# Order on TensorE in the attention steps: the product with the values of step k-1 placed behind the turning of the probabilities of step k

## The chip, the cores and the metric

One NeuronCore of a Trainium2 chip (TensorE, VectorE, ScalarE, GpSimd and SyncE, with 16 DMA engines) runs the whole kernel in one launch. The metric is device time in microseconds (us). In the profile TensorE is PE (its weight loads are PEld), VectorE is DVE, ScalarE is ACT, GpSimd is POOL and SyncE is SP. L12 is line 12 of the kernel.

## The reference

A decoder block for 256 tokens of width 1024, in float32: RMSNorm, one wide projection, a Mamba-2 mixer beside a sparse attention with 16 heads of width 64, a merge of the two by gates, an output projection, and a top-4-of-32 mixture of experts with a final RMSNorm. The part of the attention that the change touches is this:

```python
p_sel = masked_softmax(jnp.einsum('bqgrd,bgqmd->bgrqm', qb, kg), smask)
o_sel = jnp.einsum('bgrqm,bgqmd->bqgrd', p_sel.astype(vg.dtype), vg)
...
p_win = masked_softmax(jnp.einsum('bqgrd,bkgd->bgrqk', qb, kw), wmask)
o_win = jnp.einsum('bgrqk,bkgd->bqgrd', p_win.astype(vw.dtype), vw)
...
o = g[..., 0, None] * o_cmp + g[..., 1, None] * o_sel + g[..., 2, None] * o_win
```

With 256 tokens the eight chosen blocks of 64 and the window of 256 both cover all earlier tokens, so both branches are plain causal attention, with keys and values of their own.

## The kernel before

Five engines run fixed instruction streams and meet at semaphores. Up to the mixture of experts, all streams are written from one hand-made list, `token_order()`: a list of pairs (kind, number). PE, ACT, DVE and POOL each go through the whole list in its order and issue what that kind means for them; an engine that has nothing to do for a kind skips it. The place of a pair in the list therefore sets the order on four engines at once.

The attention is 16 steps k. Step k handles one tile of 128 queries (t = k // 8) and two heads. For t = 0 (k = 0 to 7) there are 128 keys, for t = 1 (k = 8 to 15) there are 256. The kinds are:

- `SC k`, the scores. PE multiplies queries and keys (L930, eight matmuls, banks 3 and 4). DVE scales, masks and takes the maxima (L1749, four custom instructions) and negates them (L1754). ACT takes the exponentials with their sums (L1342, four). PE's `SC k` waits for DVE's L1754 of `SC k-1`. The probabilities lie in one of three buffers, named TH or XDT in the rows.
- `RW k`, the row weights. DVE works out the factors from sums and gates (L1758, L1760, L1763) and POOL multiplies the probabilities with them (L661).
- `PT k`, the turning. PE transposes the probabilities (L711, four or eight matmuls) into banks 5 and 6, after POOL's L661. ACT copies bank 5 (L1350) and DVE bank 6 (L1771) into the one buffer `PTS`. PE's `PT k` also waits for both copies of step k-1.
- `PV k`, the product with the values. PE multiplies (L961 and L967) from `PTS` into bank 7. ACT writes the rounded part (L1354, OTH) and DVE the rest (L1502, OTL), which frees bank 7.
- `H u` and `P u`, the two halves of a projection unit u (24 matmuls of 256 columns each, L757 and L760), which fill PE between the attention's own instructions.
- `W u` prepares the weights of a later unit: ACT copies them rounded (L1184, WH), and POOL (L621, for the units of the merge gates and of the SSM branch) or DVE (L1472, for the others) writes what the rounding left over (WL). In these steps a `W` stands right behind an `H`.
- `GR 0` (ACT) and `GX 0` (DVE L1706, eight instructions) in steps 0 and 1, and `YS 0` (ACT L1213, DVE L1498) in step 4, finish the SSM branch.

Two waits tie `PTS` down, since it exists once. The copies of step k wait until PE has read step k-1 out of it:

```python
if k >= 1:
    act.wait_ge(pv_full, k)
a(PTS[:, 0, 0:n], psum[:, 5, 0:n], ACT.Copy).then_inc(pt_act, 1)
```

and `PV k` waits for the copies of step k (`pt_act` and `pt_dve` at k + 1) and for `pv_read` at k, the freeing of bank 7.

When the sixteenth OTL is written (`pv_read` at 16), ACT issues nine small loads (`LD 0`, L1204 to L1210) and goes on with the weights of the next units, PE starts on the NSA branch projection (`H 37`), and SP may issue the first load of expert weights (`first_load(0)`). From about 400 us to the end the mixture of experts runs, which streams 403 MB of weights.

Of the kernel before, what the change touches and what calls it, by code (L numbers as in the profile page):

```python
# [81 lines left out]
def token_order():  # L82


    u = {x: n for n, x in enumerate(UNITS)}
    out = []

    def unit(kind, m=0):
        out.extend([("H", u[(kind, m)]), ("P", u[(kind, m)])])

    for m in range(8):
        unit("xbc", m)
        if m >= 1:
            out.append(("F", m - 1))
    unit("small")
    out += [("F", 7), ("XD", 0), ("DT", 0)]
    unit("kc")
    out += [("S1", 0)]
    unit("vc")
    out += [("XT", 0)]  # L100
    unit("ks")
    out += [("XT", 1)]
    unit("kw")
    out += [("HID", 0), ("BT", 0), ("A", 0)]
    unit("vs")
    out += [("HT", 0), ("A", 1), ("XT", 2)]
    unit("vw")
    out += [("K2", 0), ("Y", 0), ("A", 2), ("ST", 0), ("XT", 3)]
    for m in range(4):
        unit("q", m)  # L110
        out += [("Y", m + 1), ("A", m + 3)]
        if m == 0:
            out += [("ST", 1)]
    unit("z", 0)
    out += [("Y", 5), ("A", 7)]
    unit("z", 1)
    out += [("Y", 6)]
    unit("z", 2)
    out += [("Y", 7), ("V2", 0), ("CT", 0), ("GY", 0)]
    unit("z", 3)  # L120
    out += [("CS", 0), ("GY", 1)]
    unit("mg", 0)
    out += [("GN", 0), ("CP", 0), ("GY", 2), ("SC", 0)]
    unit("mg", 1)
    out += [("GN", 1), ("GY", 3), ("SC", 1)]
    halves = []
    for x in [("mg", m) for m in range(2, 8)] + [("bs", m) for m in range(4)]:
        halves += [("H", u[x]), ("P", u[x])]
    out += [halves.pop(0), ("GN", 2), halves.pop(0), ("GN", 3)]
    for k in range(17):  # L130

        if k + 2 < 16:
            out.append(("SC", k + 2))
        if k < 16:
            out.append(("RW", k))
        out += {0: [("GR", 0)], 1: [("GX", 0)], 4: [("YS", 0)]}.get(k, [])
        if halves and k in (1, 8):
            out.append(halves.pop(0))
        if k >= 1:
            out.append(("PV", k - 1))  # L140
        if halves:
            out.append(halves.pop(0))
        if k < 16:
            out.append(("PT", k))
    out += halves + [("LD", 0)]
    for m in range(4):
        unit("bn", m)
        if m >= 1:
            out.append(("MT", m - 1))
    out.append(("MT", 3))  # L150
    for m in range(4):
        out.append(("H", u[("wo", m)]))
        if m:
            out.append(("XX", m - 1))
        out.append(("P", u[("wo", m)]))
        if m:
            out.append(("RM", m - 1))


    order, due = [("W", SPLIT_UNITS[SPLITS - 1])], []  # L160
    first, last = out.index(("GR", 0)), out.index(("PT", 15))
    for n, token in enumerate(out):
        order.append(token)
        if token[0] == "H" and token[1] in SPLIT_UNITS[1:]:
            i = SPLIT_UNITS.index(token[1]) - 1 + SPLITS
            if i < len(SPLIT_UNITS):
                due.append(("W", SPLIT_UNITS[i]))
        if not first <= n < last or token[0] in ("H",):
            order += due
            due = []  # L170
    return order


TOKENS = token_order()


# [1793 lines left out]
```

## Time and profile before

| | |
|---|---|
| Device time, median of 3 runs | 1339.52 us (1335.58 to 1339.84) |
| Device time of the profiled execution | 1334.48 us |
| Its span, first to last instruction | 1332.8 us |
| PE busy | 1234.6 us, 93% |
| DVE, ACT, POOL busy | 444.1, 282.3, 149.0 us |
| Mean granted PE clock | 0.981 of full speed |
| Attention steps, from the start of `PT 0` to the last OTL | 209.7 us to 336.7 us |

Busy time is the time in which an engine had an instruction in work. All places in the trace are in us from the start of the span. The profiled execution is one of its own, shorter than the median of the three runs.

### The profile page before, as it was taken

Reading aid. Unit: us, or ns where it says so; the run is one execution under the profiler, and the core shown is the slowest. Engines: PE = TensorE matmul, PEld = TensorE weight load, DVE = VectorE, ACT = ScalarE, POOL = GpSimd, SP = SyncE. Lnnn points to the kernel's source line nnn. Section 1 sums busy time; section 2 is a strip of 40 time slices with the busy share of each in tenths; the row PEclk is TensorE's granted clock in tenths of the full one; section 3 lists DMA queues with packets and bytes.
Section 4 is the critical chain, followed back from the end, with each engine's and each line's share of the span. In section 5 each row is a group of like instructions: output and inputs, shape, how many; then the busy total and the mean of one; then the engine's idle time right before and its main releaser. Section 6 shows DMA issues by size and latency. Waiting matters only on the chain.

```text
span 1332.8 us, 17482 instructions
## 1 busy us (share of the span) xinstructions
PE 1234.6 (93%) x7089; PEld 661.9 (50%) x7089; DVE 444.1 (33%) x902; ACT 282.3 (21%) x507; POOL 149.0 (11%) x101
## 2 busy tenths in 40 slices
PE   7999996898899999999999898998989899898985
PEld 7999986777884443434434233332423333232321
DVE  6965446455633131221212213121221212122113
ACT  4673444453331010101101011010101001010001
POOL 1301345353630000000000000000000000000000
PEclk9999997899999999999999999999999999999998
DMA  7747433112698999999999999999999999999994
GB/s 239 209 129 228 127 106 116 64 64 95 236 363 342 395 432 426 430 427 430 427 430 427 428 428 428 430 427 430 427 430 427 431 427 430 427 428 429 426 428 205
DMA packets 79964, 454.08 MB, mean 341 GB/s; under 512 B 10160, under 2 KB 53296, under 8 KB 55344
## 3 DMA queue, kind: packets, MB, share of 16 engines
q1 hardware_dynamic: 76960, 451.30, 82.9%
q10 hardware_dynamic: 2960, 2.17, 0.6%
q8 instruction: 31, 0.51, 0.2%
q14 instruction: 13, 0.11, 0.0%
HBM read 452.40 MB, written 1.05 MB: 340 GB/s over the span
## 4 chain that ended last, share of the span: by engine, by line
PE 60%; DMA 31%; DVE 6%; ACT 1%; issue 1%; ACTq 1%; POOL 0%; DVEq 0%; SPq 0%
DMA ring<-in_w_gate_up_dram 28%; PE psum L1043 19%; PE psum L1057 10%; PE psum L757 9%; PE psum L760 7%; PE psum L1032 5%; PE psum L1083 3%; DMA ring<-in_w_down_dram 3%; PE psum L711 2%; DVE AMX L1754 1%; PE psum L930 1%; DVE YV L1706 1%; DVE WL L1472 1%; PE psum L967 1%; PE psum L1014 1%
## 5 line engine op out<-in xcount | busy, mean ns | idle before, releaser
L1043 PE MATMUL psum<-ring,ZS 128*64 128x512 f32 x1504 | 355.2, 616 | 14.2 <-DMA ring<-in_w_gate_up_dram 14.2
L1043 PEld LDWEIGHTS psum<-ring,ZS 128*64 128x64 f32 x1504 | 100.0, 134 | 230.3 <-issue 192.5
L1906 DVE TENSOR_TENSOR X<-X,psum 128x1024 f32<-128x1024 f32 x64 | 75.3, 1217 | 388.7 <-PE psum L1083 388.7
L1057 PE MATMUL psum<-ring,HT 128*64 128x512 f32 x784 | 176.6, 596 | 20.3 <-DMA ring<-in_w_down_dram 19.6
L1890 DVE TENSOR_SCALAR ZS<-psum 128x512 f32<-128x512 f32 x32 | 22.1, 692 | 315.1 <-PE psum L1043 315.1
L1043 PE MATMUL psum<-slot,ZS 128*64 128x512 f32 x528 | 123.8, 615 | 2.0 <-DMA slot<-in_w_gate_up_dram 2.0
L1057 PEld LDWEIGHTS psum<-ring,HT 128*64 128x64 f32 x784 | 54.4, 136 | 129.9 <-issue 104.0
L1391 ACT ACTIVATE HT<-psum 128x512 f32<-128x512 f32 x32 | 19.1, 597 | 324.3 <-PE psum L711 324.3
L1472 DVE TENSOR_TENSOR WL<-ring,WH 128x2048 fp32r<-128x2048 f32 (+1 forms) x30 | 71.2, 2377 | 46.0 <-ACT WH L1184 46.0
L1184 ACT ACTIVATE WH<-ring 128x2048 fp32r<-128x2048 f32 (+1 forms) x42 | 78.5, 1873 | 10.2 <-issue 6.1
L1043 PEld LDWEIGHTS psum<-slot,ZS 128*64 128x64 f32 x528 | 35.6, 134 | 73.3 <-issue 64.7
L1032 PEld LDWEIGHTS psum<-QT,XC 128*128 128x128 f32 x512 | 63.0, 200 | 14.4 <-issue 14.4
L1032 PE MATMUL psum<-QT,XC 128*128 128x128 f32 x512 | 66.0, 289 | 1.5 <-DVEq L1829 1.5
L1083 PE MATMUL psum<-HT,QT 64*128 64x512 f32 x264 | 65.6, 615 | 1.6 <-ACT HT L1395 1.6
L1395 ACT ACTIVATE HT<-psum 128x512 f32<-128x512 f32 x32 | 19.1, 597 | 222.3 <-PE psum L1057 222.3
L621 POOL TENSOR_TENSOR WL<-ring,WH 128x2048 fp32r<-128x2048 f32 x12 | 55.2, 4603 | 41.2 <-ACT WH L1184 41.2
L1057 PE MATMUL psum<-slot,HT 128*64 128x512 f32 x240 | 54.3, 594 | 5.8 <-DMA slot<-in_w_down_dram 5.8
L1387 ACT ACTIVATE ZS<-ZS 128x512 f32<-128x512 f32 x32 | 20.2, 630 | 136.0 <-DVE ZS L1890 136.0
L757 PE MATMUL psum<-HTH,WH 128*128 128x256 f32 x320 | 47.5, 292 | 0.0
L757 PE MATMUL psum<-HTL,WH 128*128 128x256 f32 x320 | 46.2, 287 | 0.3 <-DVE HTL L1485 0.3
L757 PE MATMUL psum<-HTH,WL 128*128 128x256 f32 x320 | 45.4, 285 | 0.0
L1083 PEld LDWEIGHTS psum<-HT,QT 64*128 64x128 f32 x264 | 22.7, 186 | 45.4 <-issue 45.4
(322 smaller groups left out, 1306.6 us busy)
## 6 DMA issues: line engine op xcount, KB each, us to landing
ring<-in_w_gate_up_dram SPq DMA_DIRECT2D x94, 2048.0 KB, 33.8
ring<-in_w_down_dram SPq DMA_DIRECT2D x49, 2048.0 KB, 35.1
slot<-in_w_gate_up_dram SPq DMA_DIRECT2D x33, 2048.0 KB, 33.7
ring<-in_w_in_dram SPq DMA_DIRECT2D x30, 1024.0 KB, 5.5
slot<-in_w_down_dram SPq DMA_DIRECT2D x15, 2048.0 KB, 35.0
ring<-in_w_branch_ssm_dram SPq DMA_DIRECT2D x4, 1024.0 KB, 4.9
ring<-in_w_branch_nsa_dram SPq DMA_DIRECT2D x4, 1024.0 KB, 5.0
ring<-in_w_out_dram SPq DMA_DIRECT2D x4, 1024.0 KB, 4.9
```

The lines of the kernel that those rows point to most:

```text
L621: g.tensor_tensor(WL[i % SPLITS][:], slot_view(k, SLOT), WHF[i % SPLITS], ALU.subtract).then_inc(wl_pool, 1)
L711: return nc.tensor.transpose(o, i, IDN[:, :])
L757: ins = mm(bank(b, 2, SEQ)[:, half], w[:, k, rows], src[:, k, :], start=(n == 0 and k == 0), stop=(n == 2 and k == KT - 1))
L760: ins = mm(bank(b, 2, nco)[:, half], src[:, k, rows], w[:, k, :], start=(n == 0 and k == 0), stop=(n == 2 and k == KT - 1))
L1032: ins = mm(bank(5 + k // 4, P, off=P * (k % 4)), H2[:, t, first:first + 255:2], SPR[:, t].rearrange("p a b -> p (a b)"), start=(t == 0), s ...
L1043: ins = mm(psum[64 * (c % 2):64 * (c % 2) + 64, c // 2, :], XTS[:, k, s], every_other_pair(w[:, 2048 * (k % 2):2048 * (k % 2) + 2048], c), ...
L1057: ins = mm(psum[64 * h:64 * h + 64, 2, :], lhs, w[:, at:at + 512], start=(j + hf + k == 0), stop=(j == 1 and hf + k == 2))
L1083: ins = mm(psum[:, 3 + 2 * t + h, :], CTS[r, s, t], YSB[r, :], start=True, stop=True)
L1184: a(WH[i % SPLITS][:, 0:n], slot_view(u, n), ACT.Copy).then_inc(wh_ready, 1)
L1472: v.tensor_tensor(WL[i % SPLITS][:, 0:n], slot_view(u, n), WHF[i % SPLITS][:, 0:n], ALU.subtract).then_inc(wl_ready, 1)
L1890: v.tensor_scalar(GBU.rearrange("p (q f) -> p q f", q=2), gu[:, :, :, 0], 7.0, None, ALU.min).then_inc(g_ready, 1)
L1906: v.tensor_tensor(xo, xo, psum[:, 3 + 2 * t:5 + 2 * t, :], ALU.add).then_inc(o_read, 1)
```

## The change

In each step the pair `("PV", k - 1)` moves from before the second place of half units to behind `("PT", k)`. Nothing is added or removed, and no wait is edited.

```diff
@@ -136,12 +136,12 @@
         out += {0: [("GR", 0)], 1: [("GX", 0)], 4: [("YS", 0)]}.get(k, [])
         if halves and k in (1, 8):
             out.append(halves.pop(0))
-        if k >= 1:
-            out.append(("PV", k - 1))
         if halves:
             out.append(halves.pop(0))
         if k < 16:
             out.append(("PT", k))
+        if k >= 1:
+            out.append(("PV", k - 1))
     out += halves + [("LD", 0)]
```

A middle step k goes from `SC k+2, RW k, PV k-1, half unit (and W), PT k` to `SC k+2, RW k, half unit (and W), PT k, PV k-1`, on PE, ACT, DVE and POOL alike.

## Rows read from the trace of the kernel before

**Rows 1.** Busy time by stretch: attention steps, mixture of experts.

```profile
core 0: us, PE busy (x) PEld busy (x) DVE busy (x) ACT busy (x) POOL busy (x), PEclk, DMA share, GB/s
200.00:337.00 137.00, 111.73 (x872) 96.81 (x872) 74.83 (x221) 63.27 (x166) 60.40 (x24) 0.89 0.25 82
...
400.00:1332.80 932.80, 877.55 (x4166) 326.48 (x4166) 207.58 (x402) 92.69 (x153) 0.00 (x0) 0.99 0.98 416
```

**Rows 2.** Waits of PE, 209.7 to 337 us: total us, times, longest.

```profile
PE psum L961 <- DVE XDT L1771: 12.9, 6, 5.4
...
PE psum L711 <- POOL XDT L661: 3.9, 2, 2.1
...
PE psum L711 <- POOL TH L661: 2.2, 2, 1.7
...
PE psum L961 <- ACT XDT L1350: 0.5, 1, 0.5
```

**Rows 3.** Busy time by stretch, with the granted clock (PEclk, columns as above).

```profile
209.70:217.00 7.30, 7.26 (x38) 6.74 (x38) 5.29 (x15) 5.86 (x12) 3.16 (x1) 0.55 0.00 0
...
227.30:233.80 6.50, 6.46 (x33) 5.94 (x34) 1.60 (x13) 1.81 (x9) 1.04 (x1) 0.53 0.27 94
...
287.30:292.30 5.00, 5.00 (x34) 3.51 (x34) 2.93 (x13) 0.60 (x1) 0.00 (x0) 0.66 0.37 128
```

**Rows 4.** The chain that ended last: PE's pieces at full clock.

```profile
264.00 1.06 PE psum L930 x8
265.06 0.42 PE psum L961 x2
265.48 0.59 PE psum L967 x8
...
266.07 3.06 PE psum L760 x24
...
295.50 0.87 PE psum L711 x8
...
315.72 1.02 PE psum L967 x16
```

**Rows 5.** Timeline, step 9, and one L1754 of step 10.

```profile
279.08 1.13 PE L930 MATMUL psum<-KD,QT 64*128 64x256 f32 x8
...
280.19 4.58 POOL L621 TENSOR_TENSOR WL<-ring,WH 128x2048 fp32r<-128x2048 f32 x1 [2.18 <-ACT WH L1184]
...
281.77 3.02 DVE L1754 TENSOR_SCALAR AMX<-AMX 128x4 f32<-128x4 f32 x1
...
284.83 0.51 ACT L1342 ACTIVATE TH<-TH,AMX 128x256 f32<-128x256 f32 x1 [4.24 <-DVE AMX L1754]
...
285.35 1.89 POOL L661 TENSOR_TENSOR XDT<-XDT,AMX 128x1024 f32<-128x1024 f32 x1 [0.58 <-DVE AMX L1763]
...
287.30 1.34 PE L711 MATMUL psum<-IDN,XDT 128*128 128x128 f32 x8 [2.07 <-POOL XDT L661]
...
292.20 0.17 DVE L1754 TENSOR_SCALAR AMX<-AMX 128x4 f32<-128x4 f32 x1
```

**Rows 6.** Groups of ACT's instructions, 209.7 to 337 us: busy, mean ns.

```profile
L1184 ACT ACTIVATE WH<-ring 128x2048 fp32r<-128x2048 f32 x9 | 17.1, 1900 | 0.0
...
L1354 ACT ACTIVATE OTH<-psum 128x128 fp32r<-128x128 f32 x16 | 4.2, 261 | 5.9 <-PE psum L967 5.9
```

**Rows 7.** Timeline: the long waits, steps 2 and 5, and one copy.

```profile
227.34 0.76 PE L961 MATMUL psum<-E,ST 128*128 128x128 f32 x2 [5.41 <-DVE XDT L1771]
...
248.22 2.29 DVE L1498 TENSOR_TENSOR YSL<-YV,YSH 128x2048 fp32r<-128x2048 f32 x1 [3.04 <-ACT YSH L1213]
...
251.19 0.77 PE L961 MATMUL psum<-E,ST 128*128 128x128 f32 x2 [3.07 <-DVE XDT L1771]
...
304.77 0.60 ACT L1350 ACTIVATE XDT<-psum 128x512 f32<-128x512 f32 x1 [1.36 <-PE psum L711]
```

**Rows 8.** Timeline: the end of the attention steps.

```profile
334.54 0.46 PE L961 MATMUL psum<-E,ST 128*128 128x128 f32 x2 [0.88 <-DVE XDT L1771]
...
336.38 0.29 DVE L1502 TENSOR_TENSOR OTL<-psum,OTH 128x128 fp32r<-128x128 f32 x1 [1.99 <-ACT OTH L1354]
```

## The prediction

> **What bounds the kernel now.** I read the busy time by stretch first [rows 1]. From 400 us on the DMA engines are busy 98% of the time, so that stage moves weights at its limit; the change touches nothing in it, and its start hangs on the end of the attention: the first expert load, the nine small loads and the NSA projection all stand behind the sixteenth OTL. In the attention steps DMA is busy 25%, PE 112 us of 137, and the granted clock is 0.89. So time won or lost there goes through to the end one for one.
>
> Then I read who waits there [rows 2]. PE waits 12.9 + 0.5 us at the product (L961) for the copies of the turned probabilities, and 3.9 + 2.2 us at the turning (L711) for POOL's scaling. The change is aimed at the first kind. Two of those waits are long: 5.41 us in step 2, where DVE is held up by L1706, and 3.07 us in step 5, behind L1498 [rows 7]. Third, the clock: after the long waits the granted clock is 0.55 to 0.53, after a wait of 2.07 us it is 0.66 for 5 us [rows 3]; 0.5 is the lower of its two levels, 1.2 against 2.4 GHz. Last, the timeline of one step for the path from scores to turning [rows 5].
>
> **What the change removes.** Before, PE does `PT k-1, SC k+1, PV k-1`: only the scores (1.06 us) cover the copies, and both need at least 0.7 us (0.60 for ACT's [rows 7] and 0.1 to start). Afterwards a half unit of 3.06 us [rows 4] and the next turning stand between the copies and the product that reads them. I count the 13.4 us of L961 waits as gone; a new one at the last product is in the sum below.
>
> **What it adds.** Nothing is executed that was not before, and the bytes and issues are the same. But the product was also cover. Before, between the start of `SC k+2` and `PT k` PE has, for t = 1, 1.06 + (0.42 + 1.02) + 3.06 = 5.56 us of work [rows 4]. In that time DVE, then POOL, must finish: the scores of k+2 stand before the weights of k on DVE. From [rows 5]: scores start 279.08, L1754 issued 281.77, that is 2.69; 0.1 for L1754 when it is free; from its end (281.77 + 3.02 = 284.79) to `PT` at 287.30 is 2.51. Sum 5.3 us: just hidden before. Without the product PE has 4.12 us and waits 1.2 us. A step is then 5.3 + 0.9 (turning) + 1.44 (product) = 7.65 us against 6.5 us of PE's own work. For t = 0 the scores take 0.65, the path 3.45 and PE's cover 3.71 us: no wait.
>
> A second thing is late next. L1754, four columns wide, takes 3.02 us in step 9 and 0.17 in step 10 [rows 5]: it ends as POOL's L621 (280.19 + 4.58 = 284.77) does. L621 starts when the four exponentials (2.0 us, t = 1; 1.6, t = 0) and the copy of the weights (1.90 [rows 6]) are done, so it ends 8.6 us (t = 1; 8.2 for t = 0; 0.6 more where ACT also empties a merge-gate bank) after the last L1754. An L1754 that comes sooner waits. The Trainium skill, SBUF — State Buffer, section on the two separate sides, says so: VectorE and GpSimd share a port pair under an exclusive lock, and the loser blocks for the whole instruction. The trace agrees (3.02 against 0.17). By a model in which both only share bandwidth, steps 4, 6, 8, 9 and 11 would be up to 2 us shorter each in my sum; I go by the row.
>
> The copies of step k on ACT and DVE now wait for the product as well (`pv_full`), so they, OTH and OTL fall under the next scores. OTL is done about 1.2 us after the product: copy 0.1 to 0.7, OTH 0.26, OTL 0.29. The maxima can start 1.18 us after it. That costs nothing.
>
> **The sum, step by step.** I put the instructions one behind the other by their waits, with these durations, from the unchanged `PT 0` at 209.7.
>
> - Step 1 and 2: `P28, H29, PT1` and `PV0` now run on, `SC4` and `P29` too; PE then stands 4.3 us for L1706. `PT2` starts at 229.4 instead of 233.9: the half unit that followed the 5.41 us wait has moved under it. The slow clock comes after it as before, now on `PT2, PV1, SC5` and half of `H30`.
> - Step 3 and 4: `SC6` at 238.6 instead of 239.6. L621 (238.1 to 242.7) holds L1754, `PT4` waits 2.1 us, until 244.4 (246.4).
> - Step 5: `H31` now runs under L1498. L1754 of `SC7` ends near 250.0, `PT5` 251.6, `SC8` 253.2 instead of 258.4. Here the lead is 5.1 us.
> - Step 6: L621 runs until 258.2 and now catches the L1754 of `SC8`, which it missed before. `PT6` at 259.9 after a wait of 2.6 us, then a slow clock on `PT6, PV5, SC9`: `SC9` 262.4 instead of 263.9. Lead 1.5.
> - Step 7 to 9: `SC10` 268.5 (269.5), `SC11` 278.5 (279.1); the lock holds L1754 until 283.2, `PT9` waits 3.1 us (2.07 before), slow clock, `SC12` 288.8 (288.6). Lead gone.
> - Step 10 to 13: `SC13` 296.9 (296.3); L621 until 300.7, `PT11` waits 2.1, slow clock, `SC14` 306.1 (304.7), `SC15` 313.9 (312.7). In step 12 L1472 (2.3 us) on DVE stands before the copy of `PT12` and so before the maxima of `SC15`: `PT13` at 320.2 waits 2.1 us.
> - Step 14 to 16: without scores the path from the end of one product to the next turning is 0.1 + 0.6 + 0.26 + 0.3 (copy, OTH, OTL), 0.6 (weights) and 1.9 (L661), 3.8 us against 3.06 of half unit. `PT15` 333.0 (332.6). The last product has no cover left: 333.0 + 0.9 + 1.44 = 335.4 for `PV14`, then the copies, OTH, OTL and 0.1 before `PV15` at 336.8; before it was 334.54 [rows 8].
>
> The sixteenth OTL ends at 338.9 instead of 336.67 (336.38 + 0.29 [rows 8]): **+2.3 us**. By kinds: waits at the product -13.4, the last one +1.4, waits at the turning 21.8 us (the list above, with 0.1 to 1.0 in steps 5, 7, 8, 10, 12, 14, 15) against 6.1 [rows 2], +15.7; less some 1.4 us of slow clock, as the one behind the 3.07 us wait was the costliest. 1334.5 us of the profiled execution becomes 1336.8; it lies 5.0 us under the median of the runs, so for the median 1339.5 + 2.3 = 1341.8 us. A measurement of this kernel tells about 0.3% (4.0 us) from no change, so this is no change, on the slow side.
>
> **Bounds.** The unknown is the clock after waits of about 2 us. The trace has one of 2.07 us with 0.66 for 5 us behind it [rows 3], and 1.86 us with little slowing. I took a slow stretch of some 3.5 us behind each of the five such waits at `PT6, 9, 11, 13` and `PT4`, about 1 us each on the path (the one at `PT4` hides under L1498). If none slows, the sum is 2.3 - 4 = -1.7. If each slows for the 5.9 us that the long waits show (0.53 over 6.5 us [rows 3]), it is 1 us more on four of them, +6.
>
> **Rivals.**
>
> *Slower: the clock does not recover in steps 9 to 13.* PE's work there is 6.5 us of 7.65, with a pause in every step, where before only some steps had one. For it speaks the 0.66 behind 2.07 us [rows 3], against it that four waits of 0.9 to 1.4 us in steps 13 to 16 before stood without slowing. A slow half unit takes 5.0 instead of 3.06 us and scores, turning and product about 1.8 times their time, so a slow step is 2 + 5.0 + 1.8 + 2.5 = 11.3 us instead of 7.65. Two such steps add 7: +9, 1348.5 us. It decides from the first half step on (1.7 us over my sum is 0.3%).
>
> *Faster: the waits at the product go and those at the turning hardly grow.* Needs that DVE and POOL keep step without the product's cover. The full 13.4 us and the slow clock behind the 3.07 us wait (some 2.5 us) would give 16 us, 1323.5; more likely is that the lead of 5.1 us at `SC8` is kept, 1334.4. Against it stands the lock and the 5.3 us path [rows 5].
>
> *Lost later.* That a gain or loss of some us vanishes in the expert stage, since DMA sets its pace: it would need loads started before the end of the attention, and the first stands behind the sixteenth OTL. Then 1339.5.
>
> **How the numbers follow.** No change as worked out 0.55, lost later 0.03: 0.58 for within 0.3%. The clock rival, with all that lands over the border: 0.32, since my sum lies only 1.7 us under that border and the clock rival is beyond it. The faster rival: 0.10. The range goes from the lead kept, 1335, to the clock rival with one and a half slow steps, 1347.5.
>
> **What would show it.** Right: L961's waits near zero but for the last one of some 1.3 us; waits at L711 for L661 in nearly every step from 8 on, in the whole stage about 22 us; the 5.41 us wait gone from the product, some 4 us of it at `PT2`; the L1754 of `SC8` held to the end of an L621; `SC8` some 5 us earlier, the last OTL some 2 us later; the stages behind unchanged in length. Wrong: `PT` without waits for t = 1, or a granted clock near 0.5 through steps 9 to 13, or an expert stage of another length.

## The result, and the profile after

| | before | changed |
|---|---|---|
| Device time, median of 20 runs each | 1336.71 us | 1340.45 us |
| Ratio, 95% interval | | 1.0029 [1.0019, 1.0039] |
| Profiled execution, span | 1332.8 us | 1339.8 us |
| `PT 0` starts | 209.74 us | 213.06 us |
| From there to the end of the last OTL | 126.93 us | 130.52 us |
| From the last OTL to the end | 996.1 us | 996.2 us |

The changed kernel takes 3.7 us more. That is under what one could tell from no change by a few runs; 20 runs of each tell it. In the two profiled executions the attention steps are 3.6 us longer and the rest behind them is equal to 0.1 us. The other 3.3 us between the spans lie ahead of `PT 0`, where the change touches nothing; in new_again, the same kernel once more, `PT 0` starts at 211.5 us. I therefore count all positions below from the start of `PT 0`.

The busy time by stretch of the changed kernel, beside [rows 1]:

```profile
core 0: us, PE busy (x) PEld busy (x) DVE busy (x) ACT busy (x) POOL busy (x), PEclk, DMA share, GB/s
...
200.00:342.00 142.00, 113.64 (x883) 99.95 (x883) 73.62 (x221) 65.62 (x173) 60.98 (x25) 0.89 0.26 83
...
400.00:1339.80 939.80, 882.03 (x4201) 330.61 (x4200) 212.92 (x426) 95.95 (x164) 2.62 (x4) 0.99 0.98 416
```

The clock of the attention steps is the same 0.89 in both, and the expert stage moves the same 416 GB/s. The waits of PE from 205 to 342 us, beside [rows 2]:

```profile
PE psum L711 <- POOL XDT L661: 13.0, 8, 3.0
...
PE psum L711 <- POOL TH L661: 9.1, 5, 4.9
...
PE psum L711 <- ACT CTE L1322: 5.0, 1, 5.0
...
PE psum L961 <- DVE OTL L1502: 1.3, 1, 1.3
```

The waits at the product went from 13.4 to 1.3 us, and that 1.3 is the last product. The waits at the turning for POOL went from 6.1 to 22.1 us (the 5.0 us for ACT stands before `PT 0` in both). So a stall of 19.5 us in sum became one of 23.4 us in another place, 3.9 us more.

The timeline of the changed kernel, in order: step 2, step 6, then the later waits of PE:

```profile
233.19 1.11 PE L711 MATMUL psum<-IDN,TH 128*128 128x128 f32 x4 [4.94 <-POOL TH L661]
...
256.73 1.13 PE L930 MATMUL psum<-KD,QT 64*128 64x256 f32 x8
...
257.24 4.58 POOL L621 TENSOR_TENSOR WL<-ring,WH 128x2048 fp32r<-128x2048 f32 x1 [1.97 <-ACT WH L1184]
...
259.41 2.44 DVE L1754 TENSOR_SCALAR AMX<-AMX 128x4 f32<-128x4 f32 x1
...
262.42 1.04 POOL L661 TENSOR_TENSOR XDT<-XDT,AMX 128x512 f32<-128x512 f32 x1 [0.59 <-DVE AMX L1763]
...
263.51 1.11 PE L711 MATMUL psum<-IDN,XDT 128*128 128x128 f32 x4 [2.58 <-POOL XDT L661]
...
266.03 2.08 PE L930 MATMUL psum<-KD,QT 64*128 64x256 f32 x8
...
290.04 1.63 PE L711 MATMUL psum<-IDN,XDT 128*128 128x128 f32 x8 [3.04 <-POOL XDT L661]
...
299.28 1.09 PE L711 MATMUL psum<-IDN,XDT 128*128 128x128 f32 x8 [1.17 <-POOL XDT L661]
...
341.42 0.49 PE L961 MATMUL psum<-E,ST 128*128 128x128 f32 x2 [1.25 <-DVE OTL L1502]
```

In step 6, L621 starts 0.5 us after PE begins the scores, L1754 takes 2.44 us and ends with L621, then come the weights, L661 and the turning, and PE has stood 2.58 us. The scores behind it take 2.08 us where those before it took 1.13: the granted clock fell. Step 10 is the plain case, without an L621 in the way: 1.17 us.

### The profile page after: what moved, and what is told of

It is laid out like the page before. It is cut to its first block, busy times and chain, and to the rows that moved or that the text cites. A ratio compares the mean times of both kernels' runs of the same rounds, so it can differ in the third digit from the quotient of the medians.

```text
span 1339.8 us, 17482 instructions
## 1 busy us (share of the span) xinstructions
PE 1236.1 (92%) x7089; PEld 664.5 (50%) x7089; DVE 442.3 (33%) x902; ACT 281.9 (21%) x507; POOL 147.0 (11%) x101
## 4 chain that ended last, share of the span: by engine, by line
PE 58%; DMA 31%; DVE 7%; ACT 2%; POOL 1%; issue 1%; ACTq 0%; DVEq 0%; SPq 0%
DMA ring<-in_w_gate_up_dram 27%; PE psum L1043 19%; PE psum L1057 10%; PE psum L757 9%; PE psum L760 5%; PE psum L1032 5%; PE psum L1083 3%; DMA ring<-in_w_down_dram 3%; PE psum L711 2%; DVE AMX L1754 1%; DVE WL L1472 1%; PE psum L967 1%; DVE YV L1706 1%; PE psum L930 1%; DVE XDT L1749 1%
## 5 line engine op out<-in xcount | busy, mean ns | idle before, releaser
L1043 PE MATMUL psum<-ring,ZS 128*64 128x512 f32 x1504 | 355.3, 616 | 13.4 <-DMA ring<-in_w_gate_up_dram 13.4
L1890 DVE TENSOR_SCALAR ZS<-psum 128x512 f32<-128x512 f32 x32 | 22.1, 691 | 316.1 <-PE psum L1043 316.1
L1472 DVE TENSOR_TENSOR WL<-ring,WH 128x2048 fp32r<-128x2048 f32 (+1 forms) x30 | 72.2, 2411 | 48.4 <-ACT WH L1184 48.4
L621 POOL TENSOR_TENSOR WL<-ring,WH 128x2048 fp32r<-128x2048 f32 x12 | 55.4, 4618 | 40.1 <-ACT WH L1184 40.1
```

Source lines behind the costliest of these rows:

```text
L621: g.tensor_tensor(WL[i % SPLITS][:], slot_view(k, SLOT), WHF[i % SPLITS], ALU.subtract).then_inc(wl_pool, 1)
L1043: ins = mm(psum[64 * (c % 2):64 * (c % 2) + 64, c // 2, :], XTS[:, k, s], every_other_pair(w[:, 2048 * (k % 2):2048 * (k % 2) + 2048], c), ...
L1472: v.tensor_tensor(WL[i % SPLITS][:, 0:n], slot_view(u, n), WHF[i % SPLITS][:, 0:n], ALU.subtract).then_inc(wl_ready, 1)
L1890: v.tensor_scalar(GBU.rearrange("p (q f) -> p q f", q=2), gu[:, :, :, 0], 7.0, None, ALU.min).then_inc(g_ready, 1)
```

## How the forecast positions came out

Starts in us from the start of `PT 0` (the forecast's positions less 209.7):

| | before | forecast | changed |
|---|---|---|---|
| `PT2` | 24.2 | 19.7 | 20.1 |
| `SC6` | 29.9 | 28.9 | 29.2 |
| `PT5` | 48.1 | 41.9 | 42.3 |
| `SC8` | 48.6 | 43.5 | 43.7 |
| `PT6` | 53.7 | 50.2 | 50.4 |
| `SC10` | 59.8 | 58.8 | 60.1 |
| `SC11` | 69.3 | 68.8 | 69.7 |
| `SC12` | 78.8 | 79.1 | 80.9 |
| `SC13` | 86.6 | 87.2 | 88.5 |
| `SC15` | 102.9 | 104.2 | 104.7 |
| `PT15` | 122.9 | 123.3 | 124.8 |
| last product | 124.8 | 127.1 | 128.4 |
| last OTL, end | 126.9 | 129.2 | 130.5 |

Up to `PT6` it is within 0.4 us. The lead of 4.9 us at `SC8` is there, it is gone at `SC11`, and the rest is a loss. Behind `PT6` the forecast errs both ways: 1.1 us too short to `SC10`, 0.8 too short from `SC11` to `SC12`, 1.2 too long from `SC12` to `SC15`, 0.9 too short from there to `PT15`.

## The experiments

Every kernel was timed 5 to 12 times, beside the kernel before on the same chip, in three groups of four. Ratios are to that kernel, with their 95% intervals. "Stage" is the time from the start of `PT 0` to the end of the last OTL in the profiled execution (126.9 before, 130.5 changed). It comes from one execution each, and two of the changed kernel differ by 0.7 us.

| label | median, us | before, us | ratio | stage, us |
|---|---|---|---|---|
| new_early | 1334.61 | 1337.37 | 0.9976 [0.9962, 0.9990] | 126.6 |
| new_late | 1339.66 | 1337.37 | 1.0014 [1.0000, 1.0029] | 130.5 |
| new_warm | 1332.58 | 1337.37 | 0.9960 [0.9944, 0.9976] | 124.9 |
| new_rw12 | 1338.92 | 1337.37 | 0.9998 [0.9984, 1.0012] | 131.3 |
| new_again | 1339.29 | 1335.99 | 1.0026 [1.0013, 1.0039] | 131.2 |
| early_warm | 1331.48 | 1335.99 | 0.9963 [0.9947, 0.9978] | 123.0 |
| new_half | 1328.18 | 1335.99 | 0.9951 [0.9933, 0.9969] | 116.8 |
| old_half | 1329.12 | 1335.99 | 0.9937 [0.9910, 0.9964] | 118.1 |
| new_quart | 1329.25 | 1337.57 | 0.9941 [0.9921, 0.9961] | 122.4 |
| new_pool | 1325.92 | 1337.57 | 0.9914 [0.9892, 0.9937] | 116.0 |
| old_pool | 1325.05 | 1337.57 | 0.9911 [0.9891, 0.9931] | 115.9 |
| early_pool | 1324.37 | 1337.57 | 0.9908 [0.9887, 0.9928] | 112.7 |

**Which steps win and which lose: new_early and new_late.** The edit, against the changed kernel, with `late` as `k <= 5` in the one and `k >= 9` in the other:

```diff
+        late = k <= 5
+        if k >= 1 and not late:
+            out.append(("PV", k - 1))
         if halves:
             out.append(halves.pop(0))
         if k < 16:
             out.append(("PT", k))
-        if k >= 1:
+        if k >= 1 and late:
             out.append(("PV", k - 1))
```

> New order in steps 1 to 5, old order from step 6 on. Theory (the product behind the turning gains where a long wait for DVE stood at the product, in steps 2 and 5, and loses as cover later): the lead of 4.9 us that the changed kernel's trace has at SC8 against PT0 is won, one lock in step 6 takes some 1.7 of it, and the rest stays: the last OTL 127 - 3.2 = 124 us after the start of PT0, the kernel 3.2 us (0.2%) faster than before. Rival (only the last steps of the new order cost something, the rest is even): the lead of 4.9 us stays whole. Rival (the early steps won nothing, the trace's lead there is chance): within 1 us of before.

> Old order up to step 8, new order from step 9 on. Theory: steps 9 to 16 of the new order lack the product's cover at the turning; from SC11 to the last OTL the changed kernel's trace takes 3.2 us longer than the one before, so this kernel is 3 us (0.2%) slower than before, with waits of 3.0, 1.2, 2.1, 1.2, 2.2, 0.7 and 0.7 us at PT9 to PT15 and 1.3 us at the last product. Rival (the loss sits in steps 6 to 8): within 1 us of before.

Measured: 0.24% faster and 0.14% slower, against 0.24% and 0.2% expected. One and the same edit wins in the steps with the two long DVE jobs and loses in those of 256 keys. For new_early the times exclude the rival of chance. For new_late they don't quite exclude "within 1 us of before", since the interval begins at 1.0000; there the stage speaks, 3.6 us longer with the expected waits. In new_early `SC8` starts at 43.7 and `SC11` at 66.1 (69.3 before), the lead of 3.2 us expected and not the whole 4.9 of the other rival; its profiled execution then lost most of that to slow clock behind a wait of 2.0 us at `PT11` and to a wait of 2.35 us at PV12, so its stage is only 0.4 us shorter, while the timed runs show about 3 us. In new_late the waits from `PT10` on are those expected, with 4.0 instead of 3.0 us at `PT9`, where two orders meet.

**What the slow clock costs: new_warm.** In the changed kernel, PE does matmuls of no use while it waits at the turning:

```diff
                     else:
                         pe.wait_ge(pt_act, k)
+                    for _ in range({2: 20, 4: 7, 6: 10, 9: 12, 10: 4, 11: 8, 12: 4, 13: 8}.get(k, 0)):
+                        mm(bank(5, P), IDN[:], IDN[:], start=True, stop=True)
+                    pe.wait_ge(p_ready, k + 1)
```

> The changed kernel, with matmuls of no use (IDN by IDN, into the bank that the turning overwrites) put before the waits at the turning of steps 2, 4, 6, 9, 10, 11, 12 and 13, 20, 7, 10, 12, 4, 8, 4 and 8 of them at some 0.21 us each, a little less than each wait is long. It adds work that the reference has not, and changes no value. Theory (slow clock behind the waits costs about 8 us in the changed kernel, a good part of it on the path): granted clock near 1.0 from PT2 on, PT6, PT9 and PT13 at 0.5 to 0.9 us for their eight or four matmuls instead of 1.1 to 1.6, and 4 to 7 us less than the changed kernel, that is up to 3 us less than before. Rival (the waits alone cost, the clock is made up under the lock of L621): within 1 us of the changed kernel, 3 to 4 us above before.

Measured: 0.9960, against 1.0026 and 1.0029 for the changed kernel without them, so some 9 us less by the ratios and 5.6 us less in the stage. The busy time by stretch shows the clock, first new_warm from 205 us:

```profile
205.00:350.00 145.00, 128.07 (x1104) 116.17 (x1103) 77.55 (x218) 66.79 (x168) 64.00 (x29) 0.98 0.28 89
```

then the changed kernel, behind its waits of 4.9, 2.6, 3.0, 2.1 (`PT11`) and 2.2 us (`PT13`):

```profile
233.10:239.50 6.40, 6.31 (x35) 5.54 (x36) 2.23 (x14) 2.49 (x12) 0.85 (x2) 0.52 0.00 0
...
263.50:270.00 6.50, 6.49 (x31) 5.12 (x32) 2.49 (x13) 1.63 (x6) 0.00 (x0) 0.50 0.43 148
290.00:294.00 4.00, 3.96 (x28) 3.42 (x28) 0.00 (x0) 0.00 (x0) 0.00 (x0) 0.57 0.50 170
307.80:313.00 5.20, 5.11 (x48) 4.45 (x49) 2.52 (x12) 0.77 (x2) 0.04 (x1) 1.00 0.41 139
324.10:328.00 3.90, 3.86 (x27) 3.31 (x27) 0.00 (x0) 0.00 (x0) 0.00 (x0) 0.56 0.02 4
```

The stretches are at about the lower level, but for the one behind `PT11`, at 1.00. In new_warm the clock is 0.98 over the whole, and the rival (the waits alone cost) falls. By the timed runs the gain is more than the 4 to 7 us expected, by the stage it is within them. The difference has a place: between the last OTL and the end the profiled execution takes 992.6 us, against 996.2 in the changed kernel. Of these 3.6 us, 2.3 are waits for DVE in the projections behind the attention (1.38 and 2.63 us in the changed kernel, one of 1.68 in new_warm), and behind them the clock does not fall in new_warm. early_warm, the other kernel with such matmuls, takes 993.4 us for this part, and the twelve kernels and executions without them take 995.5 to 997.3. Why matmuls of no use inside the attention help behind it, no run here shows. So what the filled waits gave in the stage is 5.6 us, not 9.

**The path from scores to turning: new_rw12.**

```diff
+        if k < 16 and k >= 12:
+            out.append(("RW", k))
         if k + 2 < 16:
             out.append(("SC", k + 2))
-        if k < 16:
+        if k < 16 and not (k >= 12):
             out.append(("RW", k))
```

> The changed kernel, with RW k before SC k+2 in the list from step 12 on (so DVE works out the weights of step k before the maxima of the next scores, and POOL's scaling no longer waits for these). Theory (PT waits because scores, maxima, weights and scaling stand one behind the other, 5.3 us against 4.1 us of cover): the wait of 1.16 us at PT12 goes, that of 2.15 us at PT13 falls under 1 us and with it the slow clock on PT13 and PV12 (1.5 us); 3 us less than the changed kernel, within 1 us of before. Rival (POOL's own queue or the copies set the time of PT): no change against the changed kernel.

Half right. The wait at `PT12` is gone, which shows that the maxima of the next scores stood in the path. That at `PT13` grew from 2.15 to 2.75 us: the maxima came later, so did the exponentials, ACT's rounding of the next weights and DVE's L1472, and behind that the copy of `PT12`. The ratio of 0.9998 would be the 3 us expected, yet the profiled stage is 0.8 us longer than the changed kernel's, with a slow stretch behind `PT11` that the other execution had not. The wait at `PT12` is settled, the total is not.

**Do order and clock add: new_again and early_warm.** new_again is the changed kernel once more; early_warm is new_early with such matmuls in steps 0, 2, 4, 9 and 11:

```diff
+                    for _ in range({0: 20, 2: 20, 4: 7, 9: 8, 11: 7}.get(k, 0)):
+                        mm(bank(5, P), IDN[:], IDN[:], start=True, stop=True)
```

> The changed kernel once more, beside the others of this group, so that each can be set against it on the same chip: 0.2 to 0.4% above before, waits at the turning of about 22 us from step 1 on, and the last OTL about 130.5 us after the start of PT0.

> New order in steps 1 to 5, old order from step 6, and matmuls of no use before the turning in steps 0, 2, 4, 9 and 11 (20, 20, 7, 8 and 7). It adds work that the reference has not, and changes no value. Theory (order and slow clock are two costs that add): 3.2 us from the order, 1.7 behind PT0, 1.7 behind PT2 and 2.5 behind PT9 and PT11 from the clock, 9 us (0.7%) less than before, the granted clock at 1.0 through the stage. Rival (both take the same time out, since the locks of L621 follow the scores): no faster than the early order alone or the changed kernel with such matmuls, 3 to 5 us less than before.

new_again repeated the result, with 22.5 us of waits at the turning. It also shows how much a single wait moves in one and the same kernel: those at `PT5` and `PT6` are 2.20 and 1.03 us, against 0.70 and 2.58 in the other execution, with both `PT6` at 50.4 us; at `PT4`, `PT9`, `PT11` and `PT13` the two agree to 0.1 us. early_warm is a miss: 0.37% instead of 0.7%, level with new_warm. The rival holds. With PE at full clock from `PT 0`, it waits 3.04 us for POOL at `PT1` (0.29 in the changed kernel), since L661 of step 1 stands behind an L621 whose end does not depend on PE. `PT1` starts at 10.2 us in the one and at 10.0 in the other: what PE saved there it gave back at once, and behind the 3.04 us the clock fell again (0.64 over 4.7 us), where 1.0 through the whole stage was expected.

**Is it L621: new_half and old_half.**

```diff
+                    n = SLOT // 2 if k >= 32 else SLOT
+                    g.tensor_tensor(WL[i % SPLITS][:, 0:n], slot_view(k, n), WHF[i % SPLITS][:, 0:n], ALU.subtract
```

> The changed kernel, with L621 writing only the first half of the columns for units 32 to 36 (POOL's splits of steps 3, 5, 7, 8 and 10); it leaves out the rounding remainders of the other half. Theory (L621 holds L1754, and so the weights and the turning): L1754 below 0.7 us everywhere, PT4, PT6, PT9 and PT11 wait 0.5, 0, 1.1 and 1.2 instead of 2.0, 2.6, 3.0 and 2.1 us, the slow clock behind PT6 and PT9 goes too; 11 us less than the changed kernel, 7 less than before. The waits of 1.2 us for t = 1 stay. Rival (the port is not what holds L1754, and POOL's time costs nothing): within 1 us of the changed kernel.

> The kernel before with the same halved L621 (the same remainders left out). Theory: the waits at PT4, PT8, PT9 and PT11 (1.9, 0.5, 2.1, 1.7) and the slow clock behind the last two (2.5) go: 8 us less than before, about as much as the changed kernel gains from it less its own 3: so the lock costs either order something like 8 to 11 us and is not the difference between them. For t = 1 the old order then has no wait at the turning, the new one keeps 1.2 us in each step. Rival (as above): within 1 us of before.

Both are faster by about what was expected, 0.5% and 0.6%, and the intervals overlap: without a long L621 the orders are nearly level, and both were held by it. Halving takes work off POOL as well as the hold off DVE; the next experiment parts the two. The two chains then show the plain trade, free of it. new_half waits 1.16 or 1.17 us at each of `PT9` to `PT12` and never at a product but the last; at `SC15` it is 2.3 us behind old_half. It ends 1.3 us ahead largely because old_half's clock fell to 0.50 behind a wait of 2.41 us at `PV12`. old_half never waits at the turning (one line for all its waits at the product):

```profile
PE psum L962 <- DVE XDT L1772: 15.1, 6, 6.3
```

**Port or queue: new_quart.** L621 stands ahead of L661 in POOL's queue and also blocks DVE's L1754. Halving it took both away. This kernel keeps the work and cuts the hold:

```diff
+                    for q in range(4):
+                        n = slice(512 * q, 512 * q + 512)
+                        ins = g.tensor_tensor(WL[i % SPLITS][:, n], slot_view(k, SLOT)[:, n], WHF[i % SPLITS][:, n],
+                                              ALU.subtract)
+                    ins.then_inc(wl_pool, 1)
```

> The changed kernel with each L621 written as four instructions of 512 columns, the same work in sum. It separates two things that halving L621 took away at once: the port, which L621 holds for a whole instruction, and POOL's time, since L661 stands behind L621 in POOL's own queue. Theory port (as in the prediction: L621 holds L1754, and the weights and L661 wait for that): L1754 takes at most 1.2 us, the waits at PT4, PT6, PT9 and PT11 fall by 1.5 to 2.5 us each, 6 to 9 us less than the changed kernel. Rival queue (L661 could not start before the end of L621 anyway; the port adds only the 0.6 us from L1754 to L661): the waits at PT4, PT6, PT9 and PT11 fall by about 0.6 us each, the next L621 comes sooner as the exponentials do, 1 to 4 us less than the changed kernel.

Step 6 of its timeline (its lines are numbered a little higher: L623 for L621, L664 for L661, L714 for L711, L1757 for L1754):

```profile
251.22 5.00 POOL L623 TENSOR_TENSOR WL<-ring,WH 128x512 fp32r<-128x512 f32 x4 [1.96 <-ACT WH L1187]
253.75 1.27 DVE L1757 TENSOR_SCALAR AMX<-AMX 128x4 f32<-128x4 f32 x1
...
256.32 1.04 POOL L664 TENSOR_TENSOR XDT<-XDT,AMX 128x512 f32<-128x512 f32 x1
...
257.42 1.11 PE L714 MATMUL psum<-IDN,XDT 128*128 128x128 f32 x4 [2.16 <-POOL XDT L664]
```

L1754 is no longer held to the end of L621, at most 1.27 us: it slips in between two pieces. But L661 starts 0.1 us behind the last piece, and PE still waits 2.16 us (2.58 before the cut). The waits at `PT4`, `PT6`, `PT9` and `PT11` are 2.27, 2.16, 1.59 and 2.07 instead of 1.95, 2.58, 3.04 and 2.14: one of the four, `PT9`, fell nearly as the port theory has it, and three did not, so for most of the waits the rival (queue) is right. The 2.58 us at `PT6` is no firm base, since new_again waits 1.03 there; `PT4`, `PT9` and `PT11` are. The total speaks otherwise: 0.9941, some 0.9% (11 to 12 us) under the changed kernel by the ratios, more than either expected, and 8.1 us in the stage, which is what the port theory expected and twice the rival's most. In the trace it comes largely from other places: `PT2` starts 2.0 us sooner, since the eight L1706 are held less (10.2 instead of 12.7 us), and the slow clock behind it is shorter; the exponentials no longer wait, so each later L621 starts earlier; `SC12` is 8.0 us ahead. (`SC15` is 6.5 us ahead; the last 1.6 us come because the clock stayed up behind the 2.15 us at `PT13`.) It also stands 3.5 instead of 5.0 us at `PT 0`, outside the stage. How the whole divides among these I cannot say from one execution.

**Taking L621 out of the way: new_pool, old_pool, early_pool.** POOL alone does each split behind the next step's L661:

```diff
 TOKENS = token_order()
+POOL_TOKENS, held = [], []
+for token in TOKENS:
+    if token[0] == "W" and token[1] in POOL_UNITS and token[1] >= 30:
+        held.append(token)
+        continue
+    POOL_TOKENS.append(token)
+    if token[0] == "RW" and token[1] >= 1:
+        POOL_TOKENS += held
+        held = []
```

> The changed kernel with POOL doing L621 one place later in its own queue: the split of a step behind the next step's L661 instead of before it (units 30 to 36; for the first also behind RW 1, so the L1706 of the SSM branch run with a free port). ACT and PE keep the order. Theory (L621 ahead of L661, by queue and by port, is what makes PT4, PT6, PT9 and PT11 wait beyond the path of 5.3 us, and what stretches L1706 from some 3 to 12.6 us): the wait of 4.9 us at PT2 goes, PT6 and PT9 fall to 0.3 and 1.2 us; the waits of 1.2 us in steps 9 to 12 stay; 12 to 19 us less than the changed kernel, 8 to 15 less than before. Rival (an L621 that comes later holds up its own unit's half on PE, or the next L1754): within 4 us of before.

> The kernel before with POOL's L621 one place later, as in new_pool. Theory: the product's waits of 5.4 us in step 2 and the turning's of 1.9, 0.5, 2.1 and 1.7 us go, with the slow clock behind three of them; that of 3.1 us in step 5 stays or grows; 8 to 14 us less than before. Against new_pool: with POOL out of the way each step of t = 1 costs the new order its uncovered 1.2 us and the old order nothing, so the old order is level or up to 4 us ahead. Rival (the new order keeps its gain of steps 2 and 5): new_pool 3 us or more ahead.

> New order in steps 1 to 5, old from step 6, and POOL's L621 one place later. Theory: the wait of step 5 at the product goes too (3 us and its slow clock) and no turning waits for t = 1: 12 to 17 us less than before, the fastest of all, some 3 us under old_pool. Rival (once POOL is out of the way the order makes no difference in the early steps): level with old_pool.

All three are 0.9% faster than the kernel before, with everything computed. The timeline of new_pool, step 9 (L630 is L621, L670 is L661, L720 is L711, L1763 is L1754):

```profile
275.13 0.17 DVE L1763 TENSOR_SCALAR AMX<-AMX 128x4 f32<-128x4 f32 x1
...
275.86 1.89 POOL L670 TENSOR_TENSOR XDT<-XDT,AMX 128x1024 f32<-128x1024 f32 x1 [1.93 <-DVE AMX L1772]
277.71 4.54 POOL L630 TENSOR_TENSOR WL<-ring,WH 128x2048 fp32r<-128x2048 f32 x1
...
277.81 1.09 PE L720 MATMUL psum<-IDN,XDT 128*128 128x128 f32 x8 [1.16 <-POOL XDT L670]
```

L621 now runs under the turning, product and scores, L1754 is free, and what is left at the turning is the 1.16 us of the uncovered path; steps 10 to 12 have the same wait. In old_pool these steps wait 0.27 us at most at the turning; its waits are at the product:

```profile
PE psum L970 <- DVE XDT L1780: 11.2, 6, 4.2
```

The three orders cannot be told apart by time (0.9914, 0.9911, 0.9908). In the stage new_pool and old_pool are level (116.0 and 115.9) and early_pool is 3.1 us shorter, which looks like the theory and is not. Two rows say why, the stretch behind a wait of 2.5 us at `PV12`, first in old_pool, then in early_pool:

```profile
303.70:311.00 7.30, 7.29 (x43) 6.75 (x44) 2.11 (x13) 2.23 (x9) 1.89 (x1) 0.55 0.42 144
...
304.40:308.80 4.40, 4.40 (x43) 4.11 (x44) 2.10 (x13) 2.24 (x9) 1.90 (x1) 1.00 0.73 238
```

The same 43 matmuls take 2.9 us less at the full clock. From `SC9` to `SC15` early_pool is only 0.1 to 0.2 us ahead of old_pool; its whole lead stands behind this wait. So the early steps kept nothing here: the 1.4 us of lead at `SC8` went into the slow clock behind the wait at `PT5`. The rival (once POOL is out of the way, the order makes no difference there) holds. In the same way new_pool, 3.9 us behind old_pool at `SC15` by its four waits of 1.16 us, is level at the end largely by old_pool's slow stretch.

The wait of step 5 did not go either, it moved. The shift puts an L621 (238.3 to 242.9 us) against the L1498 of step 5, which now takes 4.76 us where it took 2.29 [rows 7]:

```profile
240.24 4.76 DVE L1507 TENSOR_TENSOR YSL<-YV,YSH 128x2048 fp32r<-128x2048 f32 x1 [3.04 <-ACT YSH L1222]
```

Behind it PE waits 4.70 us at `PT5` in new_pool and 4.71 in early_pool, and 4.23 at the product in old_pool. And L1706 was to fall to 3 us and fell to 8.4 (12.6 before), with 1.5 us of wait left at `PT2`. The group of new_pool's eight, with the shortest, the median and the longest in ns, shows what holds the rest:

```profile
L1715 DVE SCALAR_TENSOR_TENSOR YV<-YV,PH,CTE x8: 471/472/4837, 215.0 to 222.9; 128x256 f32<-128x256 f32 x8
```

One of the eight took 4.84 us. It ends 0.3 us behind an L621 (216.3 to 221.1 us): the L661 of step 1, behind which the split was put, is done before DVE begins the third L1706, so one L621 still falls among them.

## Why the prediction was right

- **Where the loss goes, and its size on the total.** Forecast +2.3 us and within 0.3%, measured +3.7 us, 0.29%. The stage grew by 3.6 us and the rest by nothing, as "one for one" said; the rival "lost later" is out. One for one is not a law of this kernel, though: the two kernels with matmuls of no use gained some 3 us behind the stage too.
- **What it removes.** 13.4 us of waits at the product, gone as forecast; the new one at the last product is 1.25 us against 1.4.
- **What it adds.** Forecast 21.8 us of waits at the turning, measured 22.1. The long ones are 4.9, 2.0, 2.6, 3.0, 2.1 and 2.2 us, against 4.3, 2.1, 2.6, 3.1, 2.1 and 2.1; of the short ones those in steps 10 and 12 are above the forecast's "0.1 to 1.0". The path of 5.3 us against 4.1 of cover gave 1.2 us; it is 1.17 and 1.16 in steps 10 and 12, and 1.16 in every such step of new_half and new_pool, where nothing else disturbs it.
- **The lock.** The L1754 of `SC8`, free before, was held to the end of L621, and `PT6` came 0.2 us from its place. But the step named only part of the cause. In the changed kernel both hold: L1754 waits for the port, and L661 waits for POOL itself. new_quart all but removes the first: the waits at `PT4` and `PT11` stay, that at `PT9` falls by 1.45 us, and from `PT2` on the positions move ahead, by up to 8 us. So the port is paid largely in L1706, in the exponentials and in the starts of the next L621; how it divides is not measured. The Trainium skill, SBUF — State Buffer, section on the two separate sides, has the lock held for the full instruction; cutting one instruction into four let L1754 in after at most 1.27 instead of 2.56 us, which agrees.
- **The clock, the term that was mis-sized.** By kinds the forecast had +3.7 us of waits and -1.4 us of slow clock. Measured, the waits grew by 3.9 us, and what is left of the 3.6 is -0.3: this term makes 1.1 of the 1.3 us between 2.3 and 3.6. I took some 3.5 us of slow clock behind each wait of about 2 us. Behind `PT6` it was 6.5 us at 0.50, behind `PT9` and `PT13` 4 us at 0.57 and 0.56, behind `PT11` none, which gave back 1.2 us. That the errors partly cancel is luck: in new_again the clock fell behind `PT11` too. The reading of "1.86 us with little slowing" was also off; the scores behind that wait took 1.18 us before, against 0.71 at full clock, and only the wait for L1498 hid it. The clock rival (two more slow half units from step 9 on) did not come: pauses of 0.65 to 1.17 us did not lower the clock.
- **The rival on the fast side** had its chance in the lead at `SC8`. new_early shows that most of it is real (0.9976), and new_late that the later steps lose (3.6 us in the stage, 1.0014 in time).

## What to carry to other kernels

An instruction that waits can still be cover for another one. Before moving it, add up for each later wait how much work stands between the start of its path and the wait, with and without the moved piece; here 5.56 against 5.3 us became 4.12. Where a shared list sets the order on four engines, look for the engine whose own queue holds the path: a one-place shift on GpSimd alone gave 12 us, three times what either order on TensorE was worth. Look then for what the shifted piece meets in its new place; here it doubled an L1498 and cost a wait of 4.7 us. A wait of TensorE of about 2 us often has a second price behind it, which matmuls of no use in that wait can take off when their bank is free and they fit under it. Since that price comes by chance, a difference of up to 3 us between two single traces has to be looked up by its place before it is given a cause.

## What the runs showed of the hardware

- In the twelve traces without matmuls of no use, I compared the granted clock in the 3.5 us behind each wait of PE in the attention steps. Behind all twelve waits of 2.58 to 4.23 us it was 0.50 to 0.58. Behind the 31 waits of 1.70 to 2.49 us it was 0.50 to 0.73 in 22 cases and 1.00 in nine; behind those of 1.0 to 1.6 us it was always 1.00. The middle group is chance even in one kernel: behind 2.14 us at `PT11` 1.00 in the changed kernel, behind 2.13 us there 0.60 in new_again. The profiled stage moved by 0.7 us between these two (130.5 and 131.2). Filling the waits raised the clock from 0.89 to 0.98 over the stage.
- POOL's 128x2048 subtraction took 4.58 us in one piece and 5.00 us in four, and a DVE instruction of four columns that met it took up to 3.37 us against one piece and 1.27 us against four. DVE's own 128x2048 subtraction (L1498) took 2.29 us alone and 4.76 us when POOL's had begun before it.
